# A hybrid two-block network on one core: the ring of rounded weights begins 64 bytes later

## What is computed

```
h = rms_norm(h_res, g);  z = h @ w_in
m = sigmoid(gl0)*y_a + sigmoid(gl1)*y_b + sigmoid(gl2)*y_c + sigmoid(gl3)*y_d
h_res = h_res + rms_norm(m @ w_o, g)
...
x = layer_norm(a*x + mixer(x));  x = layer_norm(a*x + (silu(x@Wg)*(x@Wu)) @ Wd)     (2 layers)
```

## The kernel before, in words

| tensor | begins at, before | modulo 256 |
|---|---|---|
| `staged` and `w_lo` | 16,512 | 128 |
| `w_hi` | 53,376 | 128 |
| `x_parts` | 114,624 | 192, then 0, 64, 128, 192, ... by chunk |
| `h_hi`, `h_lo`, `m_hi`, `m_lo`, `o_hi`, `o_lo`, `mo_hi`, `mo_lo` | 146,048 and up | 128 |
| `hidden`, `h_gate`, `up_sum` | 191,104 and up | 128 |
| `m`, `y_gated`, the `u_..._hi` and `u_..._lo` pairs | 189,696 and up | 0 |

## Time and profile before

### The profile page before, as it was taken

One profiled execution on the slowest core, in us unless ns is written; L12 is line 12 of the kernel. 1 busy time (PEld: TensorE's weight loads), 2 busy tenths in 40 slices (PEclk: granted clock), 3 DMA queues, 4 the chain that ended last, 5 costly groups with the idle time before them and its releaser, 6 DMA issues.

```text
span 862.5 us, 13049 instructions
## 1 busy us (share of the span) xinstructions
PE 850.2 (99%) x5390; PEld 757.6 (88%) x5390; DVE 629.8 (73%) x880; ACT 426.5 (49%) x613; POOL 79.3 (9%) x81
## 2 busy tenths in 40 slices
PE   8999999999999999999999999999999999999996
PEld 7998999999988987878888988889988888889885
DVE  5999857688586675796777764678987777777445
ACT  6646454456664874435444453256553544445320
POOL 0340100122003001011000000031100200000000
PEclk9999999999999999999999999999999999999998
DMA  9963776664356752557556555386544765665531
GB/s 289 270 188 92 203 203 174 181 184 123 100 169 192 238 171 86 171 169 245 184 184 193 195 186 192 117 278 195 178 142 129 244 189 183 191 195 184 187 118 50
DMA packets 121989, 154.46 MB, mean 179 GB/s; under 512 B 11663, under 2 KB 98090, under 8 KB 121930
## 3 DMA queue, kind: packets, MB, share of 16 engines
q1 hardware_dynamic: 119978, 148.23, 56.4%
q0 software_dynamic: 1872, 5.26, 1.8%
q10 hardware_dynamic: 80, 0.13, 0.0%
HBM read 151.48 MB, written 1.05 MB: 177 GB/s over the span
## 4 chain that ended last, share of the span: by engine, by line
PE 94%; DVE 4%; DMA 1%; issue 0%; ACT 0%; SPq 0%; DVEq 0%
PE acc L597 19%; PE acc L599 19%; PE acc L598 19%; PE acc L635 15%; PE acc L639 8%; PE acc L720 1%; PE acc L717 1%; PE acc L718 1%; PE acc L668 1%; PE misc L798 1%; DMA x<-in_x 1%; DVE x L2191 1%; PE misc L857 1%; DVE y L2172 1%; DMA staged<-in_moba_w_in 1%
## 5 line engine op out<-in xcount | busy, mean ns | idle before, releaser
L1709 DVE TENSOR_TENSOR w_lo<-staged,w_hi 128x1024 fp32r<-128x1024 f32 (+1 forms) x274 | 331.6, 1232 | 134.6 <-ACT w_hi L1272 134.0
L1272 ACT CAST w_hi<-staged 128x1024 fp32r<-128x1024 f32 (+1 forms) x274 | 278.0, 1044 | 90.5 <-DMA staged<-in_ffn_w_down 44.2
L597 PE MATMUL acc<-x_parts,w_hi 128*128 128x256 f32 (+2 forms) x712 | 203.4, 286 | 0.0
L598 PE MATMUL acc<-x_parts,w_hi 128*128 128x256 f32 (+2 forms) x712 | 200.6, 282 | 0.0
L599 PE MATMUL acc<-x_parts,w_lo 128*128 128x256 f32 (+2 forms) x712 | 200.5, 282 | 0.0
L635 PE MATMUL acc<-x_parts,w_hi 128*128 128x512 f32 x576 | 196.3, 393 | 0.0
L639 PE MATMUL acc<-x_parts,w_lo 128*128 128x256 f32 x576 | 149.1, 279 | 0.0
L597 PEld LDWEIGHTS acc<-x_parts,w_hi 128*128 128x128 f32 x712 | 134.4, 189 | 1.7 <-issue 1.0
L598 PEld LDWEIGHTS acc<-x_parts,w_hi 128*128 128x128 f32 x712 | 134.0, 188 | 0.7 <-issue 0.2
L599 PEld LDWEIGHTS acc<-x_parts,w_lo 128*128 128x128 f32 x712 | 134.5, 189 | 0.0
L635 PEld LDWEIGHTS acc<-x_parts,w_hi 128*128 128x128 f32 x576 | 103.3, 188 | 18.4 <-DVE gate_sum L2352 0.2
(11 more groups left out here) (394 smaller groups left out, 1256.0 us busy)
## 6 DMA issues: line engine op xcount, KB each, us to landing
staged<-in_ffn_w_gu SPq DMA_DIRECT2D x88, 512.0 KB, 3.6
staged<-in_w_in SPq DMA_DIRECT2D x58, 512.0 KB, 3.8
staged<-in_ffn_w_down SPq DMA_DIRECT2D x44, 512.0 KB, 3.3
staged<-in_gla_w_in SPq DMA_DIRECT2D x24, 512.0 KB, 4.3
staged<-in_moba_w_in SPq DMA_DIRECT2D x24, 512.0 KB, 3.9
staged<-in_w_o SPq DMA_DIRECT2D x8, 512.0 KB, 3.9
staged<-in_gla_w_out SPq DMA_DIRECT2D x8, 512.0 KB, 3.8
staged<-in_moba_w_out SPq DMA_DIRECT2D x8, 512.0 KB, 3.8
```

The costliest lines, as they stand in the source:

```text
L597: pe.matmul(dst, st_hi, mv_hi, start=start, stop=False)
L598: pe.matmul(dst, st_hi, mv_lo, start=False, stop=False)
L1272: nc.scalar.copy(hi, raw).then_inc(rounded, 1)
L1709: nc.vector.tensor_tensor(lo, raw, hi, ALU.subtract).then_inc(split, 1)
```

## The change

Between the two rings the cursor is moved on by 64 bytes:

```diff
         ring_at = cursor[0]
         staged = place("staged", [RING, SLOT])
         cursor[0] = ring_at
         w_lo = place("w_lo", [RING, SLOT], F32R)
+        cursor[0] += 64
         w_hi = place("w_hi", [RING, SLOT], F32R)
         const = place("const", CONST_N)
```

## The result

| | before | after |
|---|---|---|
| median of 20 runs each | 863.95 us (863.27 to 864.61) | 864.98 us (864.43 to 868.53) |
| ratio | | 1.0016, 95% interval 1.0010 to 1.0022 |
| profiled span | 862.5 us | 862.7 us |
| granted TensorE clock, mean of the span | 0.996 | 0.996 |

The changed kernel is slower by 1.0 us by the medians, and the interval lies wholly above 1. It is within the 0.2% that the prediction called no change, and 0.1 us from the forecast of 864.9 us. That closeness is in part luck: the forecast added 1.4 us to a median of 863.53 us over 3 runs, and over 20 runs the median of the kernel before is 863.95 us, so the added time was forecast at 1.4 us and came out at 1.0. The added line moves every later line number up by one: L597, L598 and L599 are now L598, L599 and L600, L635 is L636, L639 is L640.

A forecast was written before the change was run, and what follows sets the result against it. TensorE, busy for 99% of the span, was taken to bound the kernel. Aligned products +1.5 us and VectorE -0.1 us made +1.4 us on 863.53, so 864.9 us (chance 0.45), with a range of 862.6 to 867.0 us.

The forecast's parts named there:

- TensorE's pace is all that counts: Whole kernel: TensorE is busy for 99% of the span, and a nanosecond of mean matmul duration is one on the path.
- Distances count, not places: All operands: distances between places count, not absolute places, so only what touches `w_lo` or `staged` can change.
- Aligned products, +1.5 us: Products moving weights over `h`, `m`, `o`, `mo`: `w_lo` loses alignment, 250 x 6 ns = +1.5 us, between 0 and 3.0.
- `t_slot` and `wide_slot`, 0 with plus or minus 1.2 us: Products with `w_lo` stationary: moving chunks take each of four distances as often as before, so 0, plus or minus 1.2 us.
- The sign named as proof against the forecast: Means of L597 to L599 over `x_parts`, or of L635 and L639, shifting 2 ns or more in one direction.
- The rival of a faster `t_slot`: `t_slot`, L598 and L599: the rings' new distance gives back 2 ns each, 2.5 us, for 860.9 us; chance 0.15.
- VectorE, -0.1 us: VectorE's subtraction L1709: 16 ns less each, 4.4 us mostly hidden, -0.1 us on the path at layer borders.
- ScalarE and the DMAs, 0: ScalarE's casts keep their time, and weights still land by DMA in the unmoved `staged`: 0 for both.
- Places don't matter: Rival for the whole kernel: only VectorE's 0.1 us is left, giving 863.4 us; chance 0.20.
- Slower: Rival in the down, `m`, `o` and `mo` products: all 750 matmuls cost 4 ns more, +3.0 us, for 866.4 us; chance 0.20.
- the sign which was to decide: L597 and L599 over `h_hi` and `h_lo`: rising to 393 ns confirms the slower rival, staying at 389 to 391 refutes it.

The follow-up runs named there:

- the four fixed distances: Against the kernel before, second block's activations in 1024-byte chunks, all 0, 64, 128 or 192 from the rings: ratios 1.0022, 1.0027, 1.0027, 0.9990.

## Why the prediction was right, and where not

*TensorE's pace is all that counts, and each nanosecond of a matmul is one on the path.* Right in the sum: the time went up by 1.0 us in the medians, TensorE's busy time by 1.0, and no wait was added. Not right for each group: L639's recorded mean rose by 2 ns (279 to 281) and its pace by 0.1 (117.5 to 117.6 ns).

*Distances count, not places.* Assumed in the forecast, shown by the first two runs for the shifts they made: moving everything by 64, or the rings apart by 256, changes no group.

*Aligned products, +1.5 us.* Right in size: 2 ns on each of 750, or 1.36 us by the starts. The split was off. The forecast gave 4 ns to the `w_lo` matmul and 1 ns to each neighbour; the runs show 2, 2 and 1. Its 393 ns came out as 392, but that is a recorded duration; the pace says that more than half of the delay lands on the neighbours. And the reason given, a moving `w_lo` that meets the load of a chunk at another place, is wrong: with just that pair aligned again the kernel got slower by 2.9 us, 2.4 of it in these products by the starts. The pair of moving and own stationary operand fits the direction of all these runs, but the order within the triple only in the run that moved the low parts alone. How the delay comes about, and why one such pair costs 5 ns here and 11 ns there, stays open; the right size thus came from rows that held the effect, not from a mechanism that held.

*`t_slot` and `wide_slot`, 0 with plus or minus 1.2 us.* Right in its sum, wrong in its reason. The step that failed is to infer nothing from "each of the four distances occurs as often as before", which holds if a matmul's time hangs on its own pair alone. It doesn't, as `wide_slot` at the four fixed distances shows: `t_slot` gained 0.75 us and `wide_slot` lost 0.79, each inside the bound, and the two cancel by chance. The sign named as proof against the forecast, a shift of 2 ns or more, is there in L639's recorded mean (279 to 281 ns); by the starts it is L635's pace that grew, by 1 ns. With gaps of 128 and 192 bytes the same two groups moved by +3.2 and some -2.6 us, beyond the bound that the forecast had for 64. The rival of a faster `t_slot`, sized at 2.5 us for this gap, gave under a third of that here, and the whole of it at the gap of 192. Its reason, that a second ring at the same place slows the load, is not borne out: at the gap of 128 the rings stand apart too, and `t_slot` lost 1.8 us. The trace of before doesn't show either what was held against this rival, that the loads are not at once: in `t_slot` each is recorded with 0.19 us, and they begin 0.12 us apart (279.73, 279.85 and 279.97 us).

*VectorE, -0.1 us.* The failed term: L1709 was to lose 16 ns and lost none. It took 1239 ns after, 1235 to 1243 in the runs with other distances. The price came from the 684 ns of `m_lo`, whose inputs stand 128 apart, against the 692 of `h_lo`; with its own inputs 128 apart, in the run with that gap, L1710 took 1243 ns. So the 8 ns have another cause, which was not looked for. It cost the forecast nothing, since 0.1 us was all it was given.

*ScalarE and the DMAs, 0.* Right: casts 1046 ns against 1047; 151.48 MB read, as before.

*The rivals.* "Places don't matter" falls: by it every gap would cost the same, and the gaps of 64, 128, 192 and 256 bytes cost 1.0, 5.6, 0.7 and -0.1 us, the first two clear of zero. "Slower", with `w_hi` matmuls over `h_lo` at 393, is not seen at 64: the two `w_hi` matmuls there stand at 392 (over `h_hi`) and 389 (over `h_lo`), so that the sign which was to decide falls between its two answers. It is what the gap of 128 does (394 and 394).

## What to carry to other kernels

On a kernel that TensorE bounds, measure the pace from start to start for each kind of product, and look at the place of its operands modulo 256 bytes: give the strides of chunks and ring slots a try at multiples of 256, with one offset per kind, since the best was not the same here. Over the fixed chunks, by the starts at 0, 64, 128 and 192, moving weights took 229.1, 233.4, 232.8 and 229.9 ns, and `t_slot`, which moves 256 columns of activations, 119.9, 117.7, 119.5 and 115.1 ns. That is not a rule for every kind: `wide_slot`, which moves 512 and 256 columns of activations in turn, was quickest with chunks that walk (348.4 ns a pair against 350.8 or more). A change of place that looks neutral in the total may be a gain and a loss, as the gap of 192 was (+0.7 us in all, with `t_slot` 2.5 us quicker and the down product at 232 ns a step instead of 228); read them apart by groups, then keep the gain alone. Mixing 512- with 256-column matmuls over one pair of operands can cost more than the instructions that it saves: 348 ns for the two matmuls of a chunk here, 340 for three of 256.

## What the runs showed of the hardware that was not expected

- With weights stationary and 256 columns moving, the pace was 113.3 or 118 ns with the moving operand 192 bytes beyond the weights modulo 256, 117.8 with 64 (but for one stretch of 24 matmuls at 113.3), and 120 with equal places, at a granted clock of 1.00 in all of these stretches.
- With 512 columns of weights moving it was the other way: the pace settled at 227 ns with equal places, and a triple of the down product averaged 229 to 233 ns a step where operands stood apart.
- The same instructions at the same places ran at 113.3 or 118 ns from one stretch to the next, each stretch keeping its pace, once reached, over its 24 to 168 matmuls. With `wide_slot` ahead of them the gate columns ran at 118 ns, with three matmuls of 256 columns in its place at 113.3; stretches of the block attention differed with no 512-column matmul near.
- VectorE's subtraction showed no such dependence: 1235 to 1243 ns for 128x1024 with its two inputs 0, 64, 128 or 192 apart, and that whole range with 0 alone.
